# Attention scores as two fp32r passes over high and low parts, queries projected last

## The chip, the cores and the metric

The kernel runs on one core of one Trainium2 chip. The metric is device microseconds (us) of one execution; lower is better. The engines are TensorE (PE in the profile, its weight loads PEld), VectorE (DVE), ScalarE (ACT), GpSimd (POOL) and SyncE (SP), each with a queue of its own that it works through in order; they wait for one another by semaphores. All arithmetic results are float32. "fp32r" is a float32 operand type whose values are first rounded by the engine that writes them; a product that needs full float32 accuracy is built from several fp32r matmuls over a rounded "high" part and the remainder, the "low" part.

## The reference

One encoder layer over 1024 tokens of width 1024: a gated feed-forward half step, a token mixer, and a second feed-forward half step, each with adaptive layer norms. Only the mixer is touched by the change:

```python
proj = u @ w_in                                   # -> qA kA vA | qB kB vB, 8 heads of 64 in A and in B
# A: three dilated windows merged by their softmax denominators, per head a distance penalty
s = q @ k.T * 64 ** -0.5 + bias                   # masked outside the window
o = softmax(s) @ v
# B: 2-D neighbourhood (8 rows x 16 columns of a 16 x 64 grid), learned relative bias
out = concat([yA, yB]) @ w_out
```

## The kernel before, in words

The mixer's attention is one function, `attention_phase`, called twice: stage A for the dilated heads (tag `a`) and stage B for the neighbourhood heads (tag `b`). The eight heads of a stage are four pairs; the two heads of a pair share the 128 partitions, 64 each. A pair has 16 steps (`NU`), one for each of 8 tiles of 128 queries and each head; a stage has 64 steps (`U`).

**Projection.** The queries, keys and values of a pair are six outputs (`outputs`, L1810): part j (0 queries, 1 keys, 2 values) and half of the tokens. Each is 24 fp32r matmuls of 128x512 (`FULL`, L2203), high and low parts of weights and activations. Those of the next pair are spread over the present pair's steps, nine matmuls a step (`SPREAD`). Counting a pair's steps from 0, the outputs end in steps 2, 5, 7, 10, 13 and 15. They lie in two PSUM banks, so that output n+2 may start only when output n has been taken out (`wait_taken`). The last pair projects nothing.

**Taking an output out** (`take`, L1900) is a copy from PSUM by ACT or DVE: each takes one half of keys and values, and each one head of the queries. ACT and DVE do it in the step after the one in which the output ended (`ended_in`). The query buffer `q` holds, for each head, 64 rows of queries and 64 rows of zeros (set by POOL, L1986), so that one 128-row matmul against both heads' keys gives one head's scores. Queries and keys are double-buffered by pair.

**A step u.** PE: `score(u)`, then the transposes of the probabilities of step u-3 (`turn`, L2262), then nine projection matmuls; every eighth step the product with the values (`multiply`, L2288), and in steps 4 to 8 of a pair the transposes of its value tiles (`values`, L2230). In A a score is one float32 matmul of 128x256 over the band of keys (L2243) and four of 32x256 in column tiles of the array (L2246, "128*32" in the profile) for the strided keys `kc`; in B it is one float32 matmul of 128x384 (L2252). The profile shows each float32 matmul as two records. DVE (`step`, L2106): a reciprocal (L2119), bias and minimum (L2124), the normalisation of step u-2 from `ex` into `pn` (L2131), and then what falls due: takes, the low part of a weight (`split`, L2071), value tiles (L2079), output (L2142). ACT: the exponential (L2028, waits for the end of DVE's step), the copy of the turned probabilities of step u-3 (L2036), then takes and the high part of a weight (L2021).

**The entry of a stage** takes the first pair's outputs with nothing else running: values and keys first, then the value transposes, then the queries.

Of the kernel before, what the change touches and what calls it, by code (L numbers as in the profile page):

```python
# [1774 lines left out]
def attention_phase(nc, top, tag, w_in, w_at, w_next, y_at, ut_hi, ut_lo, scratch, ident, bias_in, tab, y_t,  # L1775
# [53 lines left out]
    def taken(n, by_vector):  # L1829

        count = 0
        for m in range(n + 1):
            j, half = outputs(m // NPJ)[m % NPJ]
            count += j == 0 or (half == 0) == by_vector
        return count

    def split_at(g, j):

        return 3 * (g - 1) + ((2, 1, 0) if g == 1 else (1, 0, 2)).index(j) + 1
# [26 lines left out]
    with ExitStack() as st:  # L1866
# [7 lines left out]
        ex = a.sb(tag + "_ex", [P, 2, W])  # L1874
        pn = a.sb(tag + "_pn", [P, 2, W])
# [6 lines left out]
        if dil:  # L1882
            v = a.sb("a_v", [P, S])
            kc = a.sb("a_kc", [P, 2, CL, CK])
            bias = a.sb("a_bias", [P, 2, A_PAD])
            y = a.sb("a_y", [P, S])[:, :]
# [13 lines left out]
        def take(p, i, eng):  # L1900


            on_vector = eng is nc.vector
            copy = nc.vector.tensor_copy if on_vector else nc.scalar.copy
            head = 0 if on_vector else 1
            j, half = outputs(p)[i]
            if j != 0 and half != head:
                return
            eng.wait_ge(pj_mm, NPJ * p + i + 1)
            out = bank(NPJ * p + i)  # L1910
            if j == 0:
                rows = slice(HD * head, HD * head + HD)
                if dil:
                    to = q[rows, p % 2, head, NB * half:NB * half + NB].rearrange("p (t r m) -> p t r m", r=CL, m=CQ)
                    of = out[rows].rearrange("p (t m r) -> p t r m", r=CL, m=CQ)
                else:
                    to = q[rows, p % 2, head, :].rearrange("p (c b r w) -> p c b r w", c=CBS, b=RBS,
                                                           r=QR)[:, :, half]
                    of = out[rows].rearrange("p (r c w) -> p c r w", r=QR, c=CBS)
                if on_vector:  # L1920
                    ins = nc.vector.tensor_scalar(to, of, -HD ** -0.5, None, ALU.mult)
                else:
                    ins = nc.scalar.activation(to, of, ACT.Copy, scale=-HD ** -0.5)
            elif j == 1:
                if dil:
                    m0 = CK // HALVES * half
                    copy(kc[:, p % 2, :, m0:m0 + CK // HALVES], out.rearrange("p (m r) -> p r m", r=CL))
                ins = copy(keys[:, p % 2, NB * half:NB * half + NB], out)
            else:
                if p >= 1:  # L1930
                    eng.wait_ge(v_tr, NVG * p)
                if dil:
                    ins = copy(v[:, NB * half:NB * half + NB], out)
                else:
                    for cb in range(CBS):
                        ins = copy(vc[:, cb, QR * half:QR * half + QR, :],
                                   out.rearrange("p (r c) -> p r c", c=COLS)[:, :, KC0[cb]:KC0[cb] + KC])
            ins.then_inc(pj_v if on_vector else pj_s, 1)

        @block.sync  # L1940
        def _(sp):
# [23 lines left out]
            for p in range(HP):  # L1965
                if p + 2 <= LAST_W:
                    for j in (1, 0, 2):
                        load_part(p + 2, j)
                if p == HP - 1 and ahead is not None:
                    sp.wait_ge(w_lo, split_at(LAST_W, 2))  # L1970
# [12 lines left out]
        def _(pool):  # L1983
            for i in range(2):
                for par in range(2):
                    nc.gpsimd.memset(q[HD * (1 - i):HD * (2 - i), par, i, :], 0.0).then_inc(zeroed, 1)  # L1986
            if dil:
                return
            pool.wait_ge(zeroed, 4)
# [27 lines left out]
        def _(act):  # L2017
# [5 lines left out]
            def exponential(u):  # L2023
# [4 lines left out]
                nc.scalar.activation(ex[:, b, :], t_s[:, b, :], ACT.Exp, bias=sm[:, b, 0:1], scale=-1.0,  # L2028
# [10 lines left out]
            take(0, 2, act)  # L2039
            split(1, 2)  # L2040
            take(0, 3, act)
            split(1, 1)
            take(0, 4, act)
            take(0, 5, act)
            for s in range(U + LAG):
# [5 lines left out]
                for g, i in ended_in(s - 1):  # L2051
                    take(g, i, act)
# [9 lines left out]
                if m == 11 and p + 2 <= LAST_W:  # L2062
                    split(p + 2, 0)
                if m == 0 and 1 <= p and p + 1 <= LAST_W:
                    split(p + 1, 2)

        @block.vector
        def _(dve):
# [37 lines left out]
            def step(u):  # L2106
# [22 lines left out]
                if u >= 4:  # L2129
                    dve.wait_ge(p_tr, u - 3)  # L2130
                nc.vector.tensor_scalar(pn[:, b, :], ex[:, b, :], sm[:, b, 2:3], None,  # L2131
                                        ALU.mult).then_inc(divided, 1)
# [19 lines left out]
            take(0, 0, dve)  # L2152
            take(0, 1, dve)
            split(1, 2)
            for g in range(NVG):
                values(0, g)
            split(1, 1)
            take(0, 4, dve)
            take(0, 5, dve)
            for s in range(U + LAG + 2):  # L2160
# [3 lines left out]
                for g, i in ended_in(s - 1):  # L2164
                    take(g, i, dve)
# [451 lines left out]
```

## Time and profile before

| | us |
|---|---|
| median of 3 runs (2078.32 to 2079.28) | 2078.88 |
| the profiled execution's own time | 2078.98 |
| its span | 2077.2 |
| PE busy | 1959.9 (94%) |
| DVE busy | 1195.8 (58%) |
| ACT busy | 801.3 (39%) |
| stage A, first score to last multiply | 797 to 1050 |
| stage B, first score to last multiply | 1093 to 1300 |

The busy share of PE counts the modelled ends of pipelined matmuls; what a matmul costs in a row of others is the distance between starts. The chain of work that ended last passes through the final feed-forward stage; for the mixer the rows below show which engine the others wait for.

### The profile page before, as it was taken

Reading aid. Unit: us, or ns where it says so; the run is one execution under the profiler, and the core shown is the slowest. Engines: PE = TensorE matmul, PEld = TensorE weight load, DVE = VectorE, ACT = ScalarE, POOL = GpSimd, SP = SyncE. Lnnn points to the kernel's source line nnn. Section 1 sums busy time; section 2 is a strip of 40 time slices with the busy share of each in tenths; the row PEclk is TensorE's granted clock in tenths of the full one; section 3 lists DMA queues with packets and bytes.
Section 4 is the critical chain, followed back from the end, with each engine's and each line's share of the span. In section 5 each row is a group of like instructions: output and inputs, shape, how many; then the busy total and the mean of one; then the engine's idle time right before and its main releaser. Section 6 shows DMA issues by size and latency. Waiting matters only on the chain. (4 is left out here: it accounts for less than half of the span.)

```text
span 2077.2 us, 27306 instructions
## 1 busy us (share of the span) xinstructions
PE 1959.9 (94%) x9962; PEld 1532.6 (74%) x9962; DVE 1195.8 (58%) x2056; ACT 801.3 (39%) x1397; POOL 606.4 (29%) x433
## 2 busy tenths in 40 slices
PE   6899999999999969999889997889999999999996
PEld 4677777777888747777567775778788888887884
DVE  5855555555686963344424445587744444457778
ACT  4533333333445363343413434336433333334541
POOL 0353444333960010000041331001543443449300
PEclk9999999999999989999999999999999999999998
DMA  9255454555874323111042220612233323367732
GB/s 318 64 192 163 163 180 160 179 166 171 317 246 144 101 62 100 30 42 41 11 106 50 41 61 31 233 71 92 95 114 102 108 95 102 117 227 264 251 99 102
DMA packets 184885, 270.56 MB, mean 130 GB/s; under 512 B 12592, under 2 KB 111152, under 8 KB 184624
## 3 DMA queue, kind: packets, MB, share of 16 engines
q1 hardware_dynamic: 153888, 235.18, 33.8%
q10 hardware_dynamic: 29840, 29.50, 4.5%
q0 software_dynamic: 1024, 4.13, 1.2%
q8 instruction: 80, 1.31, 0.3%
q14 instruction: 53, 0.43, 0.1%
HBM read 210.84 MB, written 57.93 MB: 129 GB/s over the span
## 5 line engine op out<-in xcount | busy, mean ns | idle before, releaser
L1581 PE MATMUL f_ps<-f_uh,f_ops 128*128 128x512 f32 x2496 | 783.0, 392 | 13.1 <-DVE f_ops L1272 4.2
L1581 PEld LDWEIGHTS f_ps<-f_uh,f_ops 128*128 128x128 f32 x2496 | 469.6, 188 | 127.5 <-issue 24.1
L1581 PE MATMUL f_ps<-f_ul,f_ops 128*128 128x512 f32 x1248 | 487.6, 391 | 0.0
L966 POOL TENSOR_TENSOR f_sums<-f_raw 128x512 f32<-128x512 f32 x80 | 113.0, 1413 | 547.6 <-DVE f_ul L1401 238.0
L1581 PEld LDWEIGHTS f_ps<-f_ul,f_ops 128*128 128x128 f32 x1248 | 235.0, 188 | 47.6
L1431 DVE TENSOR_TENSOR f_dl<-f_blocks,f_dh 128x1024 fp32r<-128x1024 f32 (+1 forms) x146 | 202.4, 1401 | 81.5 <-ACT f_dh L1162 81.1
L1162 ACT CAST f_dh<-f_blocks 128x1024 fp32r<-128x1024 f32 (+1 forms) x146 | 144.3, 990 | 228.2 <-PE f_ps L1715 225.6
L1715 PE MATMUL f_ps<-f_dh 128*128 128x512 f32 x496 | 196.1, 395 | 9.3 <-DVE f_ev L1465 4.9
L1272 DVE TENSOR_TENSOR f_ops<-f_sums,f_ops 128x512 fp32r<-128x512 f32 x160 | 119.6, 748 | 139.8 <-ACT f_ops L1027 139.7
L1715 PE MATMUL f_ps<-f_dh,f_dl 128*128 128x512 f32 x496 | 194.7, 393 | 0.0
L1715 PE MATMUL f_ps<-f_dl,f_dh 128*128 128x512 f32 x496 | 194.7, 393 | 0.0
L1272 DVE TENSOR_TENSOR f_ops<-f_raw,f_ops 128x512 fp32r<-128x512 f32 x136 | 106.2, 787 | 109.3 <-ACT f_ops L1027 109.2
L2203 PE MATMUL in_pj<-ut_hi,in_wh 128*128 128x512 f32 x360 | 151.6, 421 | 6.7 <-PEq L2583 4.7
L1312 DVE TENSOR_TENSOR acc<-acc,f_ps 128x512 f32<-128x512 f32 x120 | 82.4, 687 | 130.9 <-PE f_ps L1581 130.7
L2203 PE MATMUL in_pj<-ut_hi,in_wl 128*128 128x512 f32 x360 | 142.1, 395 | 0.0
L2203 PE MATMUL in_pj<-ut_lo,in_wh 128*128 128x512 f32 x360 | 141.1, 392 | 0.0
L1715 PEld LDWEIGHTS f_ps<-f_dh 128*128 128x128 f32 x496 | 94.2, 190 | 33.2 <-DVE f_dl L1431 13.8
L1715 PEld LDWEIGHTS f_ps<-f_dh,f_dl 128*128 128x128 f32 x496 | 94.1, 190 | 19.8
L1715 PEld LDWEIGHTS f_ps<-f_dl,f_dh 128*128 128x128 f32 x496 | 94.4, 190 | 19.3
L1027 ACT CAST f_ops<-f_sums 128x512 fp32r<-128x512 f32 x160 | 95.5, 618 | 33.0 <-PE f_ps L1581 17.0
L1027 ACT CAST f_ops<-f_raw 128x512 fp32r<-128x512 f32 x136 | 80.2, 620 | 40.9 <-PE f_ps L1581 17.4
L2028 ACT ACTIVATE a_ex<-a_t,a_sm 128x512 f32<-128x512 f32 x64 | 46.3, 723 | 118.2 <-DVE a_pn L2131 115.3
(249 smaller groups left out, 2987.3 us busy)
## 6 DMA issues: line engine op xcount, KB each, us to landing
f_hidden<-acc SPq DMA_DIRECT2D x154, 256.0 KB, 3.8
f_blocks<-f_hidden SPq DMA_DIRECT2D x154, 256.0 KB, 3.5
f_blocks<-in_ffn_w_down SPq DMA_DIRECT2D x132, 256.0 KB, 6.0
f_raw<-in_ffn_w_gate SPq DMA_DIRECT2D x20, 1024.0 KB, 6.1
f_raw<-in_ffn_w_up SPq DMA_DIRECT2D x20, 1024.0 KB, 5.3
f_aw<-in_w_ada ACTq DMA_DIRECT2D x28, 512.0 KB, 3.6
acc<-in_w_ada ACTq DMA_DIRECT2D x28, 512.0 KB, 4.7
in_raw<-in_w_in SPq DMA_DIRECT2D x24, 512.0 KB, 3.9
```

What stands on the lines that cost most here:

```text
L966: nc.gpsimd.tensor_tensor(sums[:, x], of, with_, how).then_inc(s_done, 1)
L1027: nc.scalar.copy(op(o)[0], source(o)).then_inc(w_hi, 1)
L1162: nc.scalar.copy(high_of(n), operands(n)).then_inc(d_hi, 1)
L1272: nc.vector.tensor_tensor(op(o)[1], source(o), op(o)[0].bitcast(F32), ALU.subtract).then_inc(w_lo, 1)
L1312: nc.vector.tensor_tensor(to, t_in, ps[:, bank, :], ALU.add).then_inc(done, 1)
L1431: nc.vector.tensor_tensor(low_of(n), operands(n), high_of(n).bitcast(F32), ALU.subtract).then_inc(d_lo, 1)
L1581: done = nc.tensor.matmul(ps[:, bank, :], l[:, k, :], r[:, k, :], start=fresh and k == 0 and m == 0, stop=closed and k == HK - 1 and m == ...
L1715: done = nc.tensor.matmul(ps[:, bank(r, t), :], left[m][:, x, P * t:P * t + P], right[m], start=r in OPENS and k == 0 and m == 0, stop=r i ...
L2028: nc.scalar.activation(ex[:, b, :], t_s[:, b, :], ACT.Exp, bias=sm[:, b, 0:1], scale=-1.0, accum_out=sm[:, b, 1:2]).then_inc(exped, 1)
L2203: done = nc.tensor.matmul(bank(n), l[:, k, j, :], r[:, k, NB * half:NB * half + NB], start=y_ == 0, stop=y_ == FULL - 1, skip_group_check= ...
```

## The change

Scores of A's band and of all of B are made of two fp32r matmuls instead of one float32 matmul. With h and l for high and low parts, the first multiplies 128 rows of q_h, stacked twice, with k_h and k_l stacked; the second multiplies the 64 rows of q_l with k_h. For this the keys have, per head, their high part in the head's own 64 rows and their low part in the other 64 (four copies of the keys instead of one, and the scale now sits on the keys); `q` holds the high part twice, and a new `q_lo` the low part of both heads. The 32x256 matmuls of A stay float32 and read a new zero-padded `q_full`. The order of a pair's projection becomes keys, values, queries. The queries are single-buffered. ACT writes the high parts first, DVE then the remainders, one step later than ACT (`ended_in(s - 2)`), and an output counts as taken when both are done. The second score half waits for the second query output separately: at step 8 in A, step 2 in B. The probabilities are normalised in place in `ex`, now three deep, and the exponential waits for the transposes of step u-3; `pn` is gone. The POOL memsets of B go away.

```diff
-        return [(j, half) for j in (1, 0, 2) for half in range(HALVES)]
+        return [(j, half) for j in (1, 2, 0) for half in range(HALVES)]
...
-            count += j == 0 or (half == 0) == by_vector
+            count += j != 2 or (half == 0) == by_vector
...
-        q = a.sb(tag + "_q", [P, 2, 2, S])
-        keys = a.sb(tag + "_k", [P, 2, S])
+        q = a.sb(tag + "_q", [P, 2, S], F32R)
+        q_lo = a.sb(tag + "_q_lo", [P, S], F32R)
+        keys = a.sb(tag + "_k", [P, 2, 2, S], F32R)
...
+                if u >= 3:
+                    act.wait_ge(p_tr, u - 2)
+                nc.scalar.activation(ex[:, u % 3, :], t_s[:, b, :], ACT.Exp, bias=sm[:, b, 0:1], scale=-1.0,
...
+                elif j == 1:
+                    for head in range(2):
+                        ins = nc.scalar.activation(keys[rows_of(head), head, p % 2, key_columns(half)],
+                                                   out[rows_of(head)], ACT.Copy, scale=-HD ** -0.5)
+                    if dil and half == 1:
+                        ins = nc.scalar.activation(class_keys(p, half), class_out(out), ACT.Copy, scale=-HD ** -0.5)
+                    ins.then_inc(pj_s, 1)
+                else:
+                    queries_free(act, p, half)
+                    for head in range(2):
+                        for rows in (rows_of(head), other_rows(head)):
+                            ins = nc.scalar.copy(query_columns(q[rows, head, :], half),
+                                                 query_out(out[rows_of(head)]))
+                    if dil:
+                        ins = nc.scalar.copy(query_columns(q_full[rows_of(1), 1, :], half), query_out(out[rows_of(1)]))
+                    ins.then_inc(pj_s, 1)
...
-                nc.vector.tensor_scalar(pn[:, b, :], ex[:, b, :], sm[:, b, 2:3], None,
-                                        ALU.mult).then_inc(divided, 1)
+                part = ex[:, (u - 2) % 3, :]
+                nc.vector.tensor_scalar(part, part, sm[:, b, 2:3], None, ALU.mult).then_inc(divided, 1)
...
+                dve.wait_ge(pj_s, taken(n, False))
+                for head in range(2):
+                    rows = rows_of(head)
+                    if j == 1:
+                        cols = key_columns(half)
+                        ins = nc.vector.scalar_tensor_tensor(keys[other_rows(head), head, p % 2, cols], out[rows],
+                                                             -HD ** -0.5, keys[rows, head, p % 2, cols].bitcast(F32),
+                                                             ALU.mult, ALU.subtract)
+                    else:
+                        ins = nc.vector.tensor_tensor(query_columns(q_lo[rows, :], half), query_out(out[rows]),
+                                                      query_columns(q[rows, head, :], half).bitcast(F32),
+                                                      ALU.subtract)
...
-            take(0, 0, dve)
-            take(0, 1, dve)
+            take(0, 0)
+            take(0, 1)
             split(1, 2)
+            take(0, 3)
             for g in range(NVG):
                 values(0, g)
...
-                for g, i in ended_in(s - 1):
-                    take(g, i, dve)
+                for g, i in ended_in(s - 2):
+                    take(g, i)
...
                 if m == 0:
+                    wait_taken(output_at(p, 0, 0))
+                if m == (NU // 2 if dil else 2):
                     wait_taken(output_at(p, 0, 1))
...
+                passes = ((slice(0, P), q[:, i, :]), (rows_of(i), q_lo[rows_of(i), :]))
+                for n, (rows, own) in enumerate(passes):
```

PE's queue in one step of stage A, as built before (`a_sc` the scores, `a_tr` the turned probabilities, `in_pj` the projection):

```order
L2243 MATMUL a_sc<-a_k,a_q 128x256
L2246 MATMUL a_sc<-a_kc,a_q 32x256 x4
L2262 MATMUL a_tr<-ident,a_pn 128x128 x4
L2203 MATMUL in_pj<-ut_hi,in_wh 128x512
L2203 MATMUL in_pj<-ut_lo,in_wh 128x512
```

and of the change:

```order
L2306 MATMUL a_sc<-a_k,a_q 128x256
L2306 MATMUL a_sc<-a_k,a_q_lo 128x256
L2316 MATMUL a_sc<-a_kc,a_q_full 32x256 x4
L2325 MATMUL a_tr<-ident,a_ex 128x128 x4
L2263 MATMUL in_pj<-ut_hi,in_wh 128x512
L2263 MATMUL in_pj<-ut_lo,in_wh 128x512
```

One matmul has become two; nothing else moved on PE within the step.

DVE's queue in stage A near the first pair's end, before: the end of step 13, step 14, and the take of the first value half. The queries had been taken four steps earlier:

```order
L2131 TENSOR_SCALAR a_pn<-a_ex,a_sm 128x512
L2119 RECIPROCAL a_sm<-a_sm 128x1
L2124 ISA a_t,a_sm<-a_sc,a_bias 128x512
L2124 ISA a_sm 128x1
L2131 TENSOR_SCALAR a_pn<-a_ex,a_sm 128x512
L1933 COPY a_v<-in_pj 128x512
```

and of the change, from the end of step 15 through steps 0 and 1 of the next pair:

```order
L2162 TENSOR_SCALAR a_ex<-a_ex,a_sm 128x512
L2202 TENSOR_TENSOR a_q_lo<-in_pj,a_q 64x512 x2
L2208 COPY a_q_full<-in_pj 64x512
L2151 RECIPROCAL a_sm<-a_sm 128x1
L2156 ISA a_t,a_sm<-a_sc,a_bias 128x512
L2156 ISA a_sm 128x1
L2162 TENSOR_SCALAR a_ex<-a_ex,a_sm 128x512
L2151 RECIPROCAL a_sm<-a_sm 128x1
L2156 ISA a_t,a_sm<-a_sc,a_bias 128x512
L2156 ISA a_sm 128x1
L2162 TENSOR_SCALAR a_ex<-a_ex,a_sm 128x512
L2202 TENSOR_TENSOR a_q_lo<-in_pj,a_q 64x512 x2
```

The query takes now stand directly ahead of the first score that reads them, and behind ACT's takes of the same outputs, which are these in ACT's queue (the second query output of the pair, then the weight split):

```order
L2064 CAST a_q<-in_pj 64x512 [waits f1_w_hi,f1_lo_b]
L2064 CAST a_q<-in_pj 64x512 x3
L2067 COPY a_q_full<-in_pj 64x512
L2024 CAST in_wh<-in_raw 128x8x128 [waits f1_lo_b,f1_tr]
L2033 ACTIVATE a_ex,a_sm<-a_t,a_sm 128x512 [waits f1_t2,f1_t5,f1_w_lo]
```

Before, ACT had one instruction for its query head there (L1923). Now it has five in A and four in B.

## Rows read from the trace of the kernel before

**Rows 1.** Windows of the two attention stages: each engine's busy time, PEclk, DMA share, GB/s.

```profile
797.00:1046.00 249.00, 237.56 (x1777) 163.25 (x1777) 110.51 (x306) 103.17 (x219) 0.00 (x0) 1.00 0.10 33
1092.00:1301.00 209.00, 195.86 (x1057) 144.16 (x1056) 98.46 (x333) 87.33 (x223) 49.37 (x54) 0.99 0.18 45
```

**Rows 2.** Timeline, one step of stage A: start, length, engine, line, operands.

```profile
855.26 0.59 PE L2243 MATMUL a_sc<-a_k,a_q 128*128 128x256 f32 x2
...
855.78 0.64 PE L2246 MATMUL a_sc<-a_kc,a_q 128*32 128x256 f32 x8
...
856.49 0.16 DVE L2119 RECIPROCAL a_sm<-a_sm 128x1 f32<-128x1 f32 x1 [1.91 <-PE a_sc L2246]
...
857.08 0.39 PE L2203 MATMUL in_pj<-ut_lo,in_wh 128*128 128x512 f32 x1
...
857.31 0.40 PE L2203 MATMUL in_pj<-ut_hi,in_wl 128*128 128x512 f32 x1
...
857.74 0.72 ACT L2028 ACTIVATE a_ex<-a_t,a_sm 128x512 f32<-128x512 f32 x1 [2.38 <-DVE a_pn L2131]
...
858.46 0.56 ACT L2036 COPY acc<-a_tr 128x512 f32<-128x512 f32 x1
...
858.93 0.59 PE L2243 MATMUL a_sc<-a_k,a_q 128*128 128x256 f32 x2
```

**Rows 3.** Timeline, one step of stage B.

```profile
1203.79 0.81 PE L2252 MATMUL b_sc<-b_k,b_q 128*128 128x384 f32 x2
...
1204.44 0.49 PE L2262 MATMUL b_tr<-ident,b_pn 128*128 128x128 f32 x3
...
1205.69 0.62 ACT L2028 ACTIVATE b_ex<-b_t,b_sm 128x384 f32<-128x384 f32 x1
...
1206.31 0.46 ACT L2036 COPY acc<-b_tr 128x384 f32<-128x384 f32 x1
...
1206.83 0.81 PE L2252 MATMUL b_sc<-b_k,b_q 128*128 128x384 f32 x2
```

**Rows 4.** Timeline, the entry of stage A.

```profile
782.55 0.59 ACT L1927 COPY a_kc<-in_pj 128x512 f32<-128x512 f32 x1 [1.66 <-PE in_pj L2203]
782.99 1.29 DVE L2079 COPY acc<-a_tr 128x512 f32<-128x512 f32 x2 [0.84 <-PE a_tr L2230]
783.04 0.59 ACT L1928 COPY a_k<-in_pj 128x512 f32<-128x512 f32 x1
...
797.53 0.67 PE L2243 MATMUL a_sc<-a_k,a_q 128*128 128x256 f32 x2 [0.82 <-DVE a_q L1921]
...
798.70 0.50 PE L2203 MATMUL in_pj<-ut_hi,in_wh 128*128 128x512 f32 x1
```

**Rows 5.** Groups of instructions: count, busy us, mean ns, idle before and its releaser.

```profile
L1312 DVE TENSOR_TENSOR acc<-acc,f_ps 128x512 f32<-128x512 f32 x120 | 82.4, 687 | 130.9 <-PE f_ps L1581 130.7
...
L2021 ACT CAST in_wh<-in_raw 128x1024 fp32r<-128x1024 f32 x21 | 22.2, 1057 | 3.3 <-DMA in_raw<-in_w_in 3.2
...
L1923 ACT ACTIVATE a_q<-in_pj 64x512 f32<-64x512 f32 x8 | 4.7, 592 | 11.7 <-PE in_pj L2203 11.6
...
L2071 DVE TENSOR_TENSOR in_wl<-in_raw,in_wh 128x1024 fp32r<-128x1024 f32 x21 | 26.9, 1282 | 12.5 <-ACT in_wh L2021 12.5
```

**Rows 6.** Timeline, fourth pair of stage A: first score and next multiply.

```profile
997.29 0.59 PE L2243 MATMUL a_sc<-a_k,a_q 128*128 128x256 f32 x2
...
1006.25 3.71 PE L2288 MATMUL mix_o<-acc 128*64 128x128 f32 x56 [0.72 <-ACT acc L2036]
```

**Rows 7.** Timeline, fourth pair of stage B: the same two.

```profile
1257.08 0.81 PE L2252 MATMUL b_sc<-b_k,b_q 128*128 128x384 f32 x2
...
1263.61 4.50 PE L2288 MATMUL mix_o<-acc 128*64 128x128 f32 x32 [0.62 <-ACT acc L2036]
```

**Rows 8.** Timeline, value transposes in step 7 of a pair of stage A.

```profile
893.93 0.75 PE L2230 MATMUL a_tr<-ident,a_v 128*128 128x128 f32 x4 [0.36 <-DVE acc L2079]
```

**Rows 9.** Window of the multiply of rows 7, columns as in rows 1.

```profile
1263.00:1268.00 5.00, 4.39 (x32) 2.99 (x32) 1.81 (x1) 1.26 (x5) 1.59 (x1) 0.66 0.01 3
```

More of the change, by code:

```diff
@@ L1898, in bank @@
             return o[:, 0, :] if bank_of(n) == 2 else pj[:, bank_of(n), :]
[L1900 to L1928, printed above, removed]
-            else:
[L1930 to L1938, printed above, removed]
@@ new lines, in key_columns, with queries_free, take_values @@
+        def key_columns(half):
+            return slice(NB * half, NB * half + NB)
+        def queries_free(eng, p, half):
+            if p >= 1:
+                last = (HT, TT)[half] if dil else (TT - 1, TT)[half]
+                eng.wait_ge(qk, NU * (p - 1) + 2 * last)
+        def take_values(p, half, eng, copy, done):
+            out = bank(output_at(p, 2, half))
+            if p >= 1:
+                eng.wait_ge(v_tr, NVG * p)
+            if dil:
+                ins = copy(v[:, NB * half:NB * half + NB], out)
+            else:
+                for cb in range(CBS):
+                    ins = copy(vc[:, cb, QR * half:QR * half + QR, :],
+                               out.rearrange("p (r c) -> p r c", c=COLS)[:, :, KC0[cb]:KC0[cb] + KC])
+            ins.then_inc(done, 1)
@@ L1940, in _, with class_keys, class_out @@
+        def class_keys(p, half):
+            m0 = CK // HALVES * half
+            return kc[:, p % 2, :, m0:m0 + CK // HALVES]
+        def class_out(out):
+            return out.rearrange("p (m r) -> p r m", r=CL)
         @block.sync
@@ L2150, in output, with take @@
                 ins.then_inc(y_out, 1)
-            take(0, 0, dve)
-            take(0, 1, dve)
+            def take(p, i):
+                j, half = outputs(p)[i]
+                if j == 2 and half == 1:
+                    return
+                n = NPJ * p + i
+                out = bank(n)
+                if j == 2:
+                    dve.wait_ge(pj_mm, n + 1)
+                    take_values(p, half, dve, nc.vector.tensor_copy, pj_v)
+                    return
+                dve.wait_ge(pj_s, taken(n, False))
[10 more added lines that the diff above has]
+                                                      ALU.subtract)
+                if dil and j == 1 and half == 0:
+                    ins = nc.vector.tensor_scalar(class_keys(p, half), class_out(out), -HD ** -0.5, None, ALU.mult)
+                if dil and j == 0:
+                    ins = nc.vector.tensor_copy(query_columns(q_full[rows_of(0), 0, :], half), query_out(out[rows_of(0)]))
+                ins.then_inc(pj_v, 1)
+            take(0, 0)
+            take(0, 1)
             split(1, 2)
+            take(0, 3)
             for g in range(NVG):
```

90 lines of the change are left out of this document (52 added, 38 removed).

## The prediction

> **What bounds the kernel now.** I read the window view by stage first. The change touches only the two attention stages, 249 and 209 us long; PE is busy for 237.6 and 195.9 us of them at full clock, DVE and ACT for less than half [rows 1]. Then the timeline of one step each. In A a step lasts 3.67 us, first score to next score (855.26 to 858.93) [rows 2]; in B 3.04 us [rows 3]. In both, DVE sits idle until PE's scores come (the 1.91 us in brackets) and ACT waits 2.38 us for DVE: for three of four pairs PE sets the pace, and what is taken off a score shortens the step. But ACT and DVE have fixed places in it, and these decide the losses. In A DVE starts 1.23 us after the step's start, ACT at 2.48, and ACT is through with its two fixed instructions at 3.76, already in the next step; DVE's fixed part ends just before ACT starts, at 2.4 [rows 2]. In B ACT runs from 1.90 to 2.98 and DVE is done by 1.9 [rows 3]. In the fourth pair, without projections, the chain PE, DVE, ACT sets the pace [rows 6, 7].
>
> **Gain: the scores.** A 512-column fp32r matmul costs 0.23 us, 857.08 to 857.31 [rows 2], so 0.45 ns a column: 0.115 us for 256 columns, 0.17 for 384. The float32 score of B costs 0.65 us for 384 columns, to the next start [rows 3]; at that rate A's 256 columns are 0.43, but 0.52 us pass before the column-tiled matmuls start [rows 2]. I read the 0.09 us between as the price of changing from the whole array to column tiles. The second new pass has 64 rows, a row tile, between passes over the whole array; no row shows such a change. Bounds: 0, or 0.09 each way. I take 0.09, as the nearest change seen.
> - A: 0.115 + 0.09 + 0.115 + 0.09 = 0.41 instead of 0.52, 0.11 less, times 64 = 7.0 us.
> - B: 0.17 + 0.09 + 0.17 + 0.09 = 0.52 instead of 0.65, 0.13 less, times 64 = 8.3 us.
>
> Sum 15.3 us. In the fourth pairs the score is a link of the chain, so I count all 64. With no row-tile change it would be 0.20 and 0.31 us each, 32.6 us; if a short pass costs as much as a 512-column one (0.23), A pays 0.55 and B 0.46 to 0.64: nothing, about -2 to +12 us.
> The Trainium skill (TensorEngine Tiling, Key Properties) says that changing the tiling mode drains the engine. The 0.09 us at 128*32 agrees with it; that it holds for row tiles no row shows. With the rule the gain is the 15.3 us taken, without it the 32.6.
>
> **Loss: the takes.** A query or key copy costs ACT 0.59 us whether it has 64 or 128 rows [rows 4, 5], and back to back they start 0.49 us apart (782.55, 783.04) [rows 4]. DVE copies go at 1.29 us for two [rows 4], and two-source ones are 0.69 each [rows 5], so 0.65 apiece. ACT's query take grows from one instruction to five in A (4 x 0.49 + 0.59 = 2.55 us) and four in B (2.06); DVE's to three (1.9) and two (1.3), and DVE now starts after ACT. The key take costs 1.1 to 1.6 us on ACT and 1.3 to 1.9 on DVE. For most outputs the next user of the bank comes 24 matmuls later, and the take still ends before it. Not so at these places:
>
> - *Entry of A, 5.0 us.* The value transposes need DVE, whose first value copy stood at 782.99 [rows 4]. Now DVE first takes the second key half, behind ACT: 782.55 + 1.57 + 1.29 = 785.4, so all that follows comes 2.4 later. At the end of the entry, PE's next projection (798.70) needs the bank of the last query output; its take began about 0.8 us before the first score (797.53, after its 0.82 us wait), at 796.75. Now: 796.75 + 2.4 + 2.55 + 1.95 = 803.7, against 798.70.
> - *Entry of B, 1.6 us.* Two ACT copies, not three: 2.0 later. The first score needs only the first query output, so its 0.8 us wait goes (as in [rows 4]); the bank there is another. ACT's and DVE's split of the next weight, queued behind, makes the first transposes wait some 0.4.
> - *Each pair's first score.* The first query output ends in step 13. ACT takes it after its fixed part of step 14, 3.6 us into it, so from 0.1 to 2.65 of step 15; DVE from 2.7 to 4.6, which is 1.1 us into the next pair's step 0, with a step of 3.5. The score waits 1.1 us: twice in A, 2.2 us. In B 2.0, then 3.3 in a step of 2.9: 0.5; and step 2 needs the second query output, which DVE finishes 6.7 us after the pair's start against 6.2: 0.6 more. Twice 1.1 = 2.2 us.
> - *The fourth pairs.* There no projection covers ACT's and DVE's work. In A: first score at 1.1, its exponential and copy to 4.75, query take to 7.3, weight split (1.06 [rows 5]) to 8.35; DVE's take from 7.35 to 9.25, its split (1.2 to 1.3 [rows 5]) to 10.5, then step 2 to 11.65; ACT's exponential and the copy on which the multiply waits end at 13.1. Before, the multiply started 8.96 after the first score [rows 6]: 4.1 us. In B, with four and two copies and no split: 9.5 against 6.53 [rows 7]: 3.0 us.
> - *Step 7.* A value transpose waits 0.36 us for DVE's value copy, which stands behind a weight split [rows 8]; B has the same order. Now two key remainders (1.29 us) stand ahead of both: 1.3 us, in two pairs of each stage, 5.2 us.
> - *Clock, 1 us.* PE now idles some 5 us before A's multiply in the fourth pair. Before B's, where it had been little busy, the granted clock was 0.66 [rows 9], between the levels of 1.2 and 2.4 GHz. A slow multiply of 3.7 us costs 0 to 3 us; I take 1.
>
> Sum: 5.0 + 1.6 + 2.2 + 2.2 + 4.1 + 3.0 + 5.2 + 1 = 24.3 us. The places are queue positions worked out; 15 to 30 covers what I may have misplaced.
>
> **Costed at nothing.** Normalising in place is the same DVE instruction. The exponential's new wait, for the transposes of step u-3, ends before DVE's fixed part does: these follow the score directly on PE, while DVE needs 1.2 us from the score. If they were held up by value copies ahead, ACT and then the copy behind it would slip, a few tenths in five steps of a pair. Without the POOL memsets B's bias loads can only start sooner. The new order of weight parts keeps SP's loads and the splits at the same steps; the query part is needed last and split last. Single-buffered queries cost a wait on scores already done when ACT gets there (step 13's by 15, step 15's by step 0).
>
> **Sum.** The profiled execution took 2078.98 us, 0.1 above the median of 2078.88, with 1.8 us around its span of 2077.2. 2078.98 - 15.3 + 24.3 = 2088.0 us.
>
> **Rivals.**
> 1. *The row tile costs no change, so the gain wins.* 2079.0 - 32.6 + 24.3 = 2070.7, faster. For it: B's score and the next projection are 0.65 us apart, so a change of operand type alone costs nothing [rows 3]. Against it: the 0.09 us at column tiles [rows 2].
> 2. *The short passes gain nothing*, because each needs a weight load that 115 ns of streaming does not hide. 2079.0 - 0 + 24.3 = 2103.3, slower still. For it: the array is loaded once per pass and the only fp32r matmuls here have 512 columns. Against: four transposes, each with a 128-column weight load of its own, start and end within 0.75 us [rows 8].
>    The Trainium skill (TensorE: Matmul & The Clock Gate, LDWEIGHTS) says a load goes by its columns, not its rows, so that the half-height pass loads no faster; no row here shows a 64-row load.
> 3. *The stalls at pair ends and step 7 do not occur* (2.2 + 2.2 + 5.2 = 9.6), the takes ending earlier than I place them: 2088.0 - 9.6 = 2078.4, no change. For it: DVE and ACT have over half of each stage free [rows 1]. Against: free time after the need is no use, and the order of the queues puts the takes just ahead of it.
>
> **Chances.** A difference of under 0.2% (4.2 us: 2074.8 to 2083.1) can't be told from none. Forecast 0.45, its own range 2082 to 2095; rival 1 0.27; rival 2 0.14; rival 3 0.14. Rival 1 ends faster unless the stalls are at their upper end, rival 3 mostly within the bound, the forecast slower but for a tenth of its weight. So faster 0.26, the same 0.18, slower 0.56. The range reaches to rivals 1 and 2: 2069 to 2102.
>
> **What would show it.** The timeline of a step in A: the column-tiled matmuls 0.41 us after the first pass, step 3.56; in B the transposes 0.52 minus the change back, some 0.43, after the first pass, step 2.91. A gap of 0.09 before the 64-row pass speaks for the forecast, none for rival 1, starts 0.2 apart for rival 2. At the entry of A, PE idle for 3.7 us after the first score. At pair starts, PE's first score waiting about 1 us for DVE's query remainder. In the fourth pair of A, 13 us from first score to multiply, less the gain. I am wrong if the steps are shorter by 0.2 us or more, or if the waits for DVE's takes are missing.

## The result and the profile after

The changed kernel takes 2124.53 us, median of 4 runs (2122.67 to 2129.33), against 2079.08 (2078.32 to 2079.68) for the kernel before: ratio 1.0222, 95% interval 1.0205 to 1.024. It is slower by 45 us; the forecast was slower by 9, and the time lies outside the range. The profiled execution took 2122.67 us with a span of 2120.9, so the spans differ by 43.7 us.

First the windows of the two stages, columns as in [rows 1], their edges moved to where the stages now lie.

```profile
797.00:1080.00 283.00, 252.83 (x1863) 177.31 (x1862) 131.10 (x333) 127.09 (x261) 1.99 (x4) 0.97 0.10 30
1114.00:1331.00 217.00, 203.88 (x1014) 145.07 (x1015) 105.70 (x323) 99.81 (x240) 50.65 (x58) 0.94 0.18 43
```

PE is idle for 30 us of stage A's window, 11 before, and the granted clock has fallen from 1.00 and 0.99 to 0.97 and 0.94. The second row is the one to remember: the idle time was forecast, the clock hardly.

Then the timeline of one step in A, the answer to [rows 2], and of one in B, the answer to [rows 3].

```profile
862.13 0.40 PE L2263 MATMUL in_pj<-ut_hi,in_wl 128*128 128x512 f32 x1
862.36 0.28 PE L2306 MATMUL a_sc<-a_k,a_q 128*128 128x256 f32 x1
862.57 0.38 PE L2306 MATMUL a_sc<-a_k,a_q_lo 64*128 64x256 f32 x1
862.88 0.64 PE L2316 MATMUL a_sc<-a_kc,a_q_full 128*32 128x256 f32 x8
...
866.03 0.28 PE L2306 MATMUL a_sc<-a_k,a_q 128*128 128x256 f32 x1
```

```profile
1173.94 0.34 PE L2311 MATMUL b_sc<-b_k,b_q 128*128 128x384 f32 x1
1174.21 0.44 PE L2311 MATMUL b_sc<-b_k,b_q_lo 64*128 64x384 f32 x1
1174.59 0.55 PE L2325 MATMUL b_tr<-ident,b_ex 128*128 128x128 f32 x3
1174.89 0.47 PE L2263 MATMUL in_pj<-ut_hi,in_wh 128*128 128x512 f32 x1
```

In A the two passes take 0.21 + 0.31 = 0.52 us, exactly what the float32 score took, and the step is 3.67 as before. In B they take 0.27 + 0.38 = 0.65, as before too, and the transposes after the 64-row pass 0.30 instead of 0.24: the step is 3.10 against 3.04 (DVE falls behind by 0.06 to 0.07 us with each step). The forecast gain of 15.3 us does not exist. TensorE's weight loads say where it went (the same step, loads only):

```profile
862.13 0.19 PEld L2306 LDWEIGHTS a_sc<-a_k,a_q 128*128 128x128 f32 x1
862.57 0.18 PEld L2306 LDWEIGHTS a_sc<-a_k,a_q_lo 64*128 64x128 f32 x1 [0.25 <-issue]
862.88 0.16 PEld L2316 LDWEIGHTS a_sc<-a_kc,a_q_full 128*32 128x32 f32 x8
```

The full-array pass of 862.36 has its weights loading from 862.13, beside the projection ahead of it. The 64-row pass of 862.57 has its load start at 862.57, with the pass itself.

The waits, where they were forecast. The entry of A (compare [rows 4]): first the value transposes of the kernel before; then, of the changed kernel, DVE's remainder, PE's value transposes, and the first projection of the next pair:

```profile
783.74 2.08 PE L2230 MATMUL a_tr<-ident,a_v 128*128 128x128 f32 x11 [0.35 <-DVE acc L2079]
```

```profile
786.02 1.39 DVE L2198 SCALAR_TENSOR_TENSOR a_k<-in_pj,a_k 64x512 fp32r<-64x512 f32 x2 [2.23 <-ACT a_kc L2058]
...
788.19 2.82 PE L2290 MATMUL a_tr<-ident,a_v 128*128 128x128 f32 x11 [3.17 <-DVE acc L2111]
...
807.44 0.76 PE L2263 MATMUL in_pj<-ut_hi,in_wh 128*128 128x512 f32 x1 [4.19 <-DVE a_q_full L2208]
```

A pair start of A; step 7 of the second pair of A (compare [rows 8]), its transposes; step 7 of a pair of B, its transposes and two projections after them; the fourth pair of A (compare [rows 6]), from its first score to the multiply; the fourth pair of B (compare [rows 7]).

```profile
871.14 0.38 PE L2306 MATMUL a_sc<-a_k,a_q 128*128 128x256 f32 x1 [1.30 <-DVE a_q_full L2208]
...
907.87 0.75 PE L2290 MATMUL a_tr<-ident,a_v 128*128 128x128 f32 x4 [2.03 <-DVE acc L2111]
...
1202.87 0.66 PE L2290 MATMUL b_tr<-ident,acc 128*128 128x128 f32 x4 [1.89 <-DVE acc L2111]
...
1204.63 0.63 PE L2263 MATMUL in_pj<-ut_lo,in_wh 128*128 128x512 f32 x1
1205.06 0.63 PE L2263 MATMUL in_pj<-ut_hi,in_wl 128*128 128x512 f32 x1
```

```profile
1015.61 0.38 PE L2306 MATMUL a_sc<-a_k,a_q 128*128 128x256 f32 x1 [1.29 <-DVE a_q_full L2208]
...
1019.37 2.35 ACT L2064 CAST a_q<-in_pj 64x512 fp32r<-64x512 f32 x4
1021.73 0.58 ACT L2067 COPY a_q_full<-in_pj 64x512 f32<-64x512 f32 x1
...
1022.35 1.39 DVE L2202 TENSOR_TENSOR a_q_lo<-in_pj,a_q 64x512 fp32r<-64x512 f32 x2 [2.67 <-ACT a_q_full L2067]
...
1026.82 1.11 PE L2325 MATMUL a_tr<-ident,a_ex 128*128 128x128 f32 x4 [5.20 <-DVE a_ex L2162]
```

```profile
1292.66 0.45 PE L2311 MATMUL b_sc<-b_k,b_q 128*128 128x384 f32 x1 [0.25 <-DVE b_q_lo L2202]
...
1299.70 0.69 PE L2311 MATMUL b_sc<-b_k,b_q 128*128 128x384 f32 x1 [4.29 <-DVE b_q_lo L2202]
```

And windows around six of these stalls, columns as before:

```profile
786.00:792.00 6.00, 3.81 (x15) 3.27 (x16) 4.97 (x8) 0.93 (x1) 0.00 (x0) 0.72 0.51 212
806.00:813.00 7.00, 5.56 (x20) 3.81 (x21) 2.12 (x7) 2.27 (x4) 0.00 (x0) 0.57 0.01 2
907.00:914.00 7.00, 6.13 (x45) 4.43 (x45) 2.85 (x9) 1.29 (x3) 0.00 (x0) 1.00 0.26 75
1026.00:1033.00 7.00, 5.93 (x61) 4.83 (x61) 1.83 (x7) 2.02 (x5) 0.00 (x0) 0.68 0.01 2
1202.00:1209.00 7.00, 6.13 (x24) 4.48 (x24) 2.56 (x9) 1.07 (x3) 0.00 (x0) 0.76 0.00 1
1299.00:1308.00 9.00, 8.29 (x43) 5.30 (x43) 2.67 (x9) 2.12 (x6) 0.44 (x1) 0.56 0.01 2
```

Five of the six are followed by a stretch at the lower of TensorE's two levels: after 1.89 us of idle in step 7 of B the projections start 0.43 us apart (1204.63, 1205.06) instead of 0.23. The sixth, 2.03 us in step 7 of A (907.87), is not, although it is the longer one: its granted clock is 1.00, and so it is behind the same stall of the next pair (979 to 987 us) and behind the pair start of 871.14. So not every stall brings a slow stretch, and its length alone doesn't say which one does. If the clock is either at its 2.4 or at its 1.2 GHz, a window of length L at mean c has spent 2(1 - c)L at the lower one and lost at most half of that, since what falls into idle time, or where PE isn't the bound, costs nothing: at most 1.7, 3.0, 2.2, 1.7 and 4.0 us here, 12.6 in all. The entry of B (0.79 from 1103 to 1111 us) adds at most 1.7, and the kernel before had 1.7 of this kind ([rows 9]), so at most some 13 us are new.

The shift of DVE's first instruction of each step, changed kernel against the one before, gives a ledger:

| place | forecast, us | measured, us |
|---|---|---|
| ahead of stage A | 0 | +1.6 |
| entry of A | +5.0 | +9.2 |
| A, pairs 1 to 3: scores; pair starts and step 7 | scores: below; +4.8 | +7.6 |
| A, fourth pair | +4.1 | +4.6 |
| entry of B | +1.6 | +3.8 |
| B, pairs 1 to 3: longer step; pair starts and step 7 | scores: below; +4.8 | +3 and +5.8 |
| B, fourth pair | +3.0 | +6.8 |
| behind B | 0 | +1.3 |
| clock | +1 | in the rows above |
| scores | -15.3 | 0, and the +3 of B above |
| sum | +9.0 | +43.7 |

### The profile page after: what moved, and what is told of

Read it like the earlier page. It is cut to its first block and busy times, and to the rows that moved or that the text cites. A ratio compares the mean times of both kernels' runs of the same rounds, so it can differ in the third digit from the quotient of the medians.

```text
span 2120.9 us, 27326 instructions
## 1 busy us (share of the span) xinstructions
PE 1980.1 (93%) x9962; PEld 1545.3 (73%) x9962; DVE 1230.8 (58%) x2104; ACT 846.9 (40%) x1477; POOL 598.7 (28%) x427
## 5 line engine op out<-in xcount | busy, mean ns | idle before, releaser
L2000 POOL DMA_DIRECT2D b_runs<-bias_table x32 | 16.2, 515 | 299.4 <-POOLq L2647 298.6
```

What stands on the lines that cost most here:

```text
L2000: pool.dma_start(runs[QC * rr:QC * rr + QC, :, 0:RUN], tab[:, 2 * p:2 * p + 2, at:at + RUN]).then_inc(r_ld, 16)
```

## The experiments

The ratio of each run is to the kernel before, timed beside it. Differences in us between two runs are those of their medians; worked out from the ratios they come out up to 3 us larger or smaller.

**Two parts of the change alone.** Normalisation in place, on the kernel before:

```diff
-        ex = a.sb(tag + "_ex", [P, 2, W])
-        pn = a.sb(tag + "_pn", [P, 2, W])
+        ex = a.sb(tag + "_ex", [P, 3, W])
...
+                if u >= 3:
+                    act.wait_ge(p_tr, u - 2)
```

> The kernel before with nothing but the normalisation in place: three buffers of exponentials instead of two and two of normalised ones. Theory: this part of the change is worth nothing, 2077-2081. Rival (the exponential waits for the transposes of three steps before, and loses time after a stall, or the engine reads and writes one buffer more slowly): 2084 or more, with ACT's wait for the transposes shown.

Measured 2080.5 us, ratio 0.9999 (0.999 to 1.0009): worth nothing, as expected. The order of the projections, on the kernel before:

```diff
-        return [(j, half) for j in (1, 0, 2) for half in range(HALVES)]
+        return [(j, half) for j in (1, 2, 0) for half in range(HALVES)]
...
-                for g, i in ended_in(s - 1):
+                for g, i in ended_in(s - 2):
                     take(g, i, dve)
```

> The kernel before with float32 scores and double-buffered queries, but the projections of a pair in the order keys, values, queries, and DVE's copies one step later, as in the changed kernel. Theory (the order alone puts the last query copy at the pair's end, but one plain copy on each engine is short): 2079-2085, the pair starts and the fourth pairs together at most 6 us later. Rival (the order alone makes the stalls of the pair starts, of the fourth pairs and of step 7): 2090-2100.

Measured 2080.9 us, ratio 0.9998 (0.9989 to 1.0007). Queries last cost nothing while a take is one instruction per engine. What is left for the 45 us are the scores and the takes: these are longer, DVE's wait for ACT's, and the queries have one buffer. The last point, and POOL's dropped memsets, no run takes by themselves.

**The second pass.** Left out:

```diff
-                passes = ((slice(0, P), q[:, i, :]), (rows_of(i), q_lo[rows_of(i), :]))
+                passes = ((slice(0, P), q[:, i, :]),)
```

> The changed kernel without the second pass: the product of the low parts of the queries with the high parts of the keys is left out, the rest (remainders included) stays. With the run of the second pass over all rows it tells what a pass costs and what the change of rows costs. Theory: a pass over all rows costs 0.11-0.17, so this is a further 0.11 x 64 + 0.17 x 64 = 18 us below the run with whole-array passes, about 2080 (2070-2088); a pass over 64 rows costs 0.31 in A and 0.37 in B. Rival (the score's time isn't on the path): 2118-2126.

Measured 2085.6 us, ratio 1.0024 (1.0015 to 1.0034): 39 us below the changed kernel, for 128 second passes. That is 0.30 us each. In the steps it is more in B than the pass itself: a score falls from 0.52 to 0.21 us in A (855.77 to 855.98 in its trace) and from 0.65 to 0.18 in B (1132.14 to 1132.32), since the first pass then no longer stands before another shape; in the fourth pairs, where PE isn't the bound, it is less.

The pass made over all rows comes next. A form of it with zeros in the other head's rows needs twice the space for the low query parts and did not fit in SBUF, so it has no time. The one below leaves the other head's low parts in place:

```diff
-                passes = ((slice(0, P), q[:, i, :]), (rows_of(i), q_lo[rows_of(i), :]))
+                passes = ((slice(0, P), q[:, i, :]), (slice(0, P), q_lo))
```

> The changed kernel with its second pass over all 128 rows instead of its head's 64, on the same q_lo tile: the other head's rows of q_lo meet this head's low key parts, a product of two remainders some 2^-24 of the score, so nothing is zeroed and nothing else changes. Theory (the change to 64 rows and back and the load that the 64-row pass cannot hide eat what the missing passes save): from the first matmul of a score to its end 0.52 becomes 0.32-0.36 in stage A, 0.64 becomes 0.34-0.42 in stage B; 0.18 x 64 + 0.26 x 64 = 28 us off the changed kernel: 2097 (2090-2104); the one-pass run at 2085.6 leaves 0.11 to 0.17 a pass for it. Rival (a second pass costs 0.3 whatever its rows): 2120-2126.

Measured 2097.1 us, ratio 1.0077 (1.0062 to 1.0092): 27.4 us off the changed kernel by making the matmul twice as tall. It is 11.5 us above the run with one pass, where 18 had been expected; the steps account for some 15 (3.47 against 3.33 in A, 2.76 against 2.59 in B), and the rest is open. Timelines of a step in A, matmuls, then loads, and of one in B:

```profile
855.60 0.28 PE L2306 MATMUL a_sc<-a_k,a_q 128*128 128x256 f32 x1
855.72 0.28 PE L2306 MATMUL a_sc<-a_k,a_q_lo 128*128 128x256 f32 x1
855.92 0.64 PE L2316 MATMUL a_sc<-a_kc,a_q_full 128*32 128x256 f32 x8
...
855.37 0.19 PEld L2306 LDWEIGHTS a_sc<-a_k,a_q 128*128 128x128 f32 x1
855.60 0.19 PEld L2306 LDWEIGHTS a_sc<-a_k,a_q_lo 128*128 128x128 f32 x1
...
1130.68 0.34 PE L2311 MATMUL b_sc<-b_k,b_q 128*128 128x384 f32 x1
1130.86 0.34 PE L2311 MATMUL b_sc<-b_k,b_q_lo 128*128 128x384 f32 x1
1131.04 0.49 PE L2325 MATMUL b_tr<-ident,b_ex 128*128 128x128 f32 x3
```

0.12 + 0.20 = 0.32 in A, 0.18 + 0.18 = 0.36 in B. The load of the second pass now starts 0.12 us ahead of it, and the starts are no further apart than the 0.115 and 0.17 us that the columns take to stream. The first pass of the changed kernel costs 0.09 us more before the 64-row pass (0.21) than before the same pass at full height (0.12), and the pass ahead of the column-tiled matmuls shows that price too (0.20 instead of 0.12). In the other order, on the changed kernel:

```diff
-                passes = ((slice(0, P), q[:, i, :]), (rows_of(i), q_lo[rows_of(i), :]))
+                passes = ((rows_of(i), q_lo[rows_of(i), :]), (slice(0, P), q[:, i, :]))
```

> The changed kernel with its two passes in the other order: the 64-row pass (low query parts by high key parts) first, then the pass over all rows. It tells the two causes of the 64-row pass's price apart. If the price is the change of rows alone (one change in, one out, wherever the pass stands), each score costs the same and the whole is 2122-2126. If it is the weight load that can't be hidden beside a pass of another shape, then the load of the 64-row pass now stands behind the last projection (more idle before the score) and the load of the full pass behind the 64-row pass: the same count of bare loads, 2122-2128 as well, but in A the step from the second pass to the class products falls from 0.31 to 0.22, and the time turns up ahead of the score. Rival (the end of the 64-row pass was slow only because the column-tiled class products or the transposes come next): 5 us or more faster, 2110-2119.

Measured 2144.0 us, ratio 1.0312 (1.0284 to 1.034): 19.5 us slower still, which none of the three foresaw. Its timeline in A, and in B:

```profile
864.67 0.39 PE L2263 MATMUL in_pj<-ut_hi,in_wl 128*128 128x512 f32 x1
864.99 0.38 PE L2306 MATMUL a_sc<-a_k,a_q_lo 64*128 64x256 f32 x1
865.30 0.38 PE L2306 MATMUL a_sc<-a_k,a_q 128*128 128x256 f32 x1
865.61 0.64 PE L2316 MATMUL a_sc<-a_kc,a_q_full 128*32 128x256 f32 x8
...
864.99 0.18 PEld L2306 LDWEIGHTS a_sc<-a_k,a_q_lo 64*128 64x128 f32 x1 [0.35 <-issue]
865.30 0.19 PEld L2306 LDWEIGHTS a_sc<-a_k,a_q 128*128 128x128 f32 x1
...
1162.46 0.44 PE L2311 MATMUL b_sc<-b_k,b_q_lo 64*128 64x384 f32 x1
1162.83 0.45 PE L2311 MATMUL b_sc<-b_k,b_q 128*128 128x384 f32 x1
1163.12 0.49 PE L2325 MATMUL b_tr<-ident,b_ex 128*128 128x128 f32 x3
...
1162.83 0.19 PEld L2311 LDWEIGHTS b_sc<-b_k,b_q 128*128 128x128 f32 x1 [0.19 <-issue]
```

In A the last projection takes 0.32 us to the next start (0.23 otherwise), and both passes take 0.31, each with its load starting together with it, and each before yet another shape. The full pass of B separates the two prices: it is the first of its shape, with its load bare, but the transposes behind it have its shape, and it takes 0.29 us instead of 0.18. So one rule covers the three kernels. A pass costs its streaming, 0.11 us in A and 0.17 to 0.18 in B, where its own load ran ahead and the next instruction has its shape; 0.09 to 0.10 more when the next has another shape; and 0.11 more when it is itself the first of its shape, since its load doesn't run ahead. The 0.31 is 0.11 + 0.11 + 0.09. For A that gives 0.20 + 0.31 = 0.51 in the changed kernel (measured 0.52), 0.11 + 0.20 = 0.31 at full height (0.32) and 0.09 + 0.31 + 0.31 = 0.71 here; for B 0.27 + 0.38 = 0.65 in the changed kernel, behind which the transposes, first of their shape again, take another 0.06. Whether the 0.11 is the bare load or something else in entering a shape, the rows can't tell; the two always come together.

The step is 3.86 us for 3.67 in A and 3.16 for 3.10 in B, 12 of the 19.5 us over 48 steps each; the granted clock of A's window is 0.93 instead of 0.97, and the rest was not taken apart. My miscount was to take the loads as equally many: in A, with the low pass between projection and full pass, two score passes stand bare, not one.

**The takes.** DVE's remainders left out, on the full-height version (low parts stay zero):

```diff
-                for head in range(2):
...
+                if not dil or (j == 1 and half == 1):
+                    dve.wait_ge(pj_v, taken(n, True) - 1)
+                    dve.sem_inc(pj_v, 1)
+                    return
```

> The run with whole-array passes without DVE's remainders: the low parts of keys and queries are zeroed once by POOL and stay zero (the products with low parts are left out in effect), ACT's casts, the float32 copies, both passes, order, banks and waits stay. It tells whether the remainders on DVE or the casts on ACT cost what the stalls cost. Theory (the stalls at the entries, pair starts, step 7 and in the fourth pairs are DVE's 1.4 us remainders in series behind ACT): 20 to 28 us off 2097.1, 2069-2077. Rival (ACT's four casts a query half are what delays, the remainders only happen to end last): at most 10 us off, 2087 or more.

Measured 2071.3 us, ratio 0.9957 (0.9943 to 0.9972): 25.8 us for 64 instructions of 0.69 us, what the waits behind them do to the clock included; of their 44 us of DVE time less than half had been covered. The first of the two entry edits:

```diff
-            take(0, 3)
             for g in range(NVG):
                 values(0, g)
+            take(0, 3)
```

> The run with whole-array passes plus the first of the two entry edits alone: DVE's key remainder of the second half behind its copies of the first value transposes, the banks as in the changed kernel. It divides the 16.2 us that both edits gave. Theory (3.2 us of idle at the value transposes, then some 3.5 us at the lower clock level, and a smaller part in B; the other half is the projection behind the last query take): 6 to 9 us off 2097.1, so 2088-2091. Rival (one of the two edits gives it all): 2096-2097 or 2081-2083.

Measured 2087.0 us, ratio 1.0033 (1.0021 to 1.0046): 10.1 us off, just more than the 6 to 9 expected. Both entry edits:

```diff
-            return (0, 1, 2, 0, 1, 0)[n]
+            return (0, 1, 2, 0, 2, 1)[n]
```

> The run with whole-array passes plus two edits at the entry of a stage: DVE's key remainder of the second half behind its copies of the first value transposes, and the two query projections in the banks 2 and 1 instead of 1 and 0, so that the next pair's first projection waits for an earlier take. Theory (entry A's 9.2 us are the value transposes behind the remainder, the projection behind the last query take, and the cold clock behind each): 7-9 us off in A and 2-3 in B, about 2086 (2084-2090). Rival (the entry is bound by the sum of ACT's and DVE's takes before the first score): at most 3 us off, 2094 or more.

Measured 2080.9 us, ratio 1.0003 (0.9993 to 1.0012): 16.2 us off, more than the 7 to 13 of the expected range. The two waits at the entry of A in the runs with one edit and with both:

```profile
784.61 2.08 PE L2290 MATMUL a_tr<-ident,a_v 128*128 128x128 f32 x11 [0.35 <-DVE acc L2111]
802.82 0.76 PE L2263 MATMUL in_pj<-ut_hi,in_wh 128*128 128x512 f32 x1 [4.39 <-DVE a_q_full L2208]
```

```profile
785.96 2.08 PE L2290 MATMUL a_tr<-ident,a_v 128*128 128x128 f32 x11 [0.35 <-DVE acc L2111]
...
799.68 0.50 PE L2263 MATMUL in_pj<-ut_hi,in_wh 128*128 128x512 f32 x1
```

The first edit takes the 3.17 us before the transposes away, the second the 4.39 before the projection, and the window of 797 to 857 us goes from a granted clock of 0.94 to 1.00. The idle time that the two edits remove at A is 7.2 us; the rest of the 16 must be clock and B's entry, which no run separates. Next, on top of both, DVE's value copies ahead of takes and splits:

```diff
+                if values_due(s - 1):
+                    values(*values_due(s - 1))
                 for g, i in ended_in(s - 2):
                     take(g, i)
```

> The run before this one plus DVE's copies of the value transposes ahead of its takes and weight splits in each step. Theory (the transposes of step 7 wait behind remainder and split, with a cold clock after it): 6 stalls of 1.3 to 1.9 us plus 1 to 2 us of cold clock in some, 6-9 us off the run with the entry edits. Rival (the remainder that is now later is waited for instead, by the projection that needs its bank): no change within 2 us.

Measured 2072.9 us, ratio 0.9959 (0.9944 to 0.9975): 8.1 us off, as expected. And the query projections finished sooner:

```diff
-    SPREAD = 9
+    SPREAD = [9] * 12 + [12] * 3 + [0]
+    DONE = [sum(SPREAD[:m]) for m in range(17)]
```

> The run before this one plus another spread of the projections: 9 matmuls in each of the first 12 steps, 12 in the next three and none in the last, in place of 9 in all 16; the first query half ends a step earlier and the second two steps. Theory (pair starts wait 1.3 us for the first half's remainder, and the fourth pair opens with the last take on ACT and DVE uncovered, 3.6 and 4.4 us of it): 6 x 1.1 = 6 us and 4 to 6 us off, some 10 in all. Rival (the longer steps 12 to 14 and the empty step 15 lose what the takes gain, since the take then stands in a step without projections): within 2 us of the run before, or slower.

Measured 2065.4 us, ratio 0.9927 (0.9911 to 0.9944): 7.5 us off, a little under the 10 expected; PE's wait for the first query remainder at pair starts (1.3 to 1.5 us each) is gone. The control with float32 scores and the same edits (the one on DVE's key remainder has nothing to act on there):

> A control for the four stacked edits: the kernel before with its float32 scores and plain double-buffered copies, the order keys, values, queries, and all the edits of the early-queries run (banks 2 and 1 at the entry, DVE's copies of the value transposes ahead of its takes, the spread 9, 12, 0). Theory (the two passes over all rows are worth some 31 us in the score groups and give back most of it in takes; what the edits gain they gain mostly by hiding those takes): 2073-2079, so the early-queries run's 2065.4 is faster than this one by 8 to 14. Rival (the edits alone are what makes that version fast, and the two passes are worth nothing net): 2062-2067.

Measured 2076.6 us, ratio 0.9989 (0.9979 to 0.9999). So the edits do little for the kernel that has no long takes, and the two passes are worth some 11 us once their second pass is full-height and their takes are covered. Last, the query take divided over two steps, its copies for the other rows read from SBUF:

```diff
+                        for head in range(2):
+                            ins = nc.scalar.copy(query_columns(q[other_rows(head), head, :], half),
+                                                 query_columns(q[rows_of(head), head, :], half).bitcast(F32))
```

> The early-queries run plus a lighter last query take: ACT rounds the two own halves and copies its float32 part, and a semaphore then lets DVE begin, while ACT makes the two copies for the other rows from SBUF, one step later in the loop; DVE's float32 copy comes a step later too. Theory (at the start of the fourth pair nothing covers ACT's 2.9 us and DVE's 2.1 us; steps there wait 4.6 us for DVE in A and 3.1 in B): 1 to 2 us off at each of both fourth pairs and 1 us at each entry, 3 to 5 us in all, 2060-2062. Rival (the copies from SBUF or the later ones are then waited for by the first scores): within 1 us of 2065.4 or slower.

Measured 2062.4 us (2058.3 to 2066.6), ratio 0.9918 (0.9895 to 0.994): the fastest, 0.8% below the kernel before. Its interval overlaps with that of the run before it (0.9911 to 0.9944), so that this last edit gains anything is likely but not shown; the wait it aimed at is shorter in the fourth pair of A (4.64 us in the run before):

```profile
996.96 1.12 PE L2348 MATMUL a_tr<-ident,a_ex 128*128 128x128 f32 x4 [2.76 <-DVE a_ex L2174]
```

## Why the prediction was wrong

The direction was right and the time too low: 2088.0 against 2122.67 us of the profiled execution, 34.7 us. In the ledger's terms 18.3 of them are the scores (15.3 forecast as gained, 3 lost), 13.5 the stalls with the clock behind them, and 2.9 lie ahead of A and behind B, where nothing was forecast.

- **The gain of 15.3 us, the step that failed.** "I take 0.09, as the nearest change seen." What it took is right: the pass before the 64-row one costs 0.21 and not 0.11, and the 64-row pass pays the same again on its own way out. But "0.115 + 0.09 + 0.115 + 0.09 = 0.41" has one price for each change, and there are two. The first matmul of a new shape also starts together with its weight load, and that term, which stands only in rival 2, was put at nothing in the sum. It measures 0.11 us, for the full pass of B in the run with the low pass first (0.29 - 0.18) and for the 64-row pass of A here (0.31 - 0.115 - 0.09). With it the forecast's own sum gives 0.41 + 0.11 = 0.52 in A (measured 0.52) and 0.52 + 0.11 = 0.63 in B (0.65), and B's transposes behind the pass take 0.06 more. That is as much as the passes left out saved: the gain is 0 in A and -3 us in B. The row it came from, [rows 2], could not show it: in the kernel before the only such changes are those to and from the column-tiled matmuls, where such a price would be inside their 0.57 us and the transposes behind. The full-height run shows that nothing else was wrong with the term: a score is 0.20 us shorter in A (0.52 to 0.32) and 0.29 in B (0.65 to 0.36), where 0.20 and 0.31 had been worked out for passes without that change.
- **Rival 2 had the time's reason half right.** Its figure, 2103.3, assumed that any short pass waits for its load. The full-height passes are 0.12 us apart with loads recorded at 0.19, so that is false; here only a load across a change of shape waits. Its chance was put at 0.14, on four transposes of one shape, [rows 8], which say nothing on a change.
- **The stalls and the clock behind them, the other failed step.** The waits stood where they were placed: 3.17 and 4.19 us at the entry of A (2.4 and 2.6 of net delay foreseen), 1.30 at pair starts (1.1), 2.03 in step 7 of A (1.3 and the 0.36 there before) and 1.89 and 0.64 in that of B, and 12.6 from first score to multiply in A's fourth pair (1015.61 to 1028.18; 13 foreseen). But the stalls in the ledger sum to 37.8 us against 23.3 foreseen and 1 for the clock. The largest excesses are the entry of A (4.2), B's fourth pair (3.8) and the entry of B (2.2), and the windows there are at the lower level for a part (0.72 and 0.57, 0.56, and 0.79 from 1103 to 1111 us). I had priced the clock once, at the one place where the kernel before showed it, [rows 9], and not behind every stall that might bring it. The 2.8 us of excess in pairs 1 to 3 of A are not clock, which is at 1.00 behind those waits: they are five shifts of 1.5 us, the fifth the start of the fourth pair, which the forecast had under that pair, and the others each 0.2 to 0.4 longer than foreseen. How the excess at the other places divides between clock and waits is argued from the windows, not measured.
- **Costed at nothing, and right:** the in-place normalisation (ratio 0.9999), the order of projections and DVE's later step (0.9998). What POOL's dropped memsets and the single-buffered queries are worth no run shows.
- **Rivals 1 and 3** fell: no step became shorter, and every forecast wait occurred.

A sum of measured terms, with one remainder: the full-height run has steps 0.20 us shorter in A and 0.28 in B (3.47 and 2.76), 23 us over 48 steps each. Remainders cost 25.8. That leaves 14 for everything else in the change, ACT's casts and the float32 copies above all: -23 + 26 + 14 = +17, the full-height run; +27 for the 64 rows gives +44. The 14 is what is left, not measured by itself.

The Trainium skill (TensorEngine Tiling, Key Properties) says that a change of tiling mode drains the engine; the trace agrees, with 0.09 to 0.10 us on the matmul ahead of the change. A second statement of the Trainium skill (TensorE: Matmul & The Clock Gate, The mechanism) is that a weight load overlaps matmuls under way only when its row group differs; the same section also lets a load into a background weight buffer run ahead. As it stands the "only" doesn't hold here: loads of the same 128*128 shape and the same rows ran ahead of their pass (855.60 for 855.72). The load for the 64-row tile, whose rows are among those of the full-array pass ahead of it, did not (862.57 for 862.57). The measurement decides.

## What to carry to other kernels

A short matmul in another tile shape between full ones pays for the change on both sides and, with its load not running ahead, 0.11 us more: in all 0.20 us a step more than the same matmul padded to the full array where column tiles follow anyway (A), 0.34 where its neighbours are full-array ones on both sides (B). Pad it, with rows whose product is negligible if there are any. Look at the granted clock behind each new stall of PE: several here brought a slow stretch worth up to 4 us, and stalls of 1.3 and 2.0 us none. And put the long take behind the short copy that PE waits for.

## What the runs showed of the hardware

- A 256-column fp32r pass over the whole array costs 0.11 to 0.12 us among its like; one over 64 rows between other shapes 0.31, nearly three times as much for half the rows.
- In the run with the low pass first, both passes of A cost 0.31, the 64-row one and the full one: it is the change that counts, not the height. Leaving a shape costs 0.09 to 0.10 us, entering one 0.11 (0.29 instead of 0.18 for the full pass of B), or 0.06 where three transposes follow (0.30 instead of 0.24).
- After 1.89 us of PE idle behind a stretch of normal work, the projections from 1204.63 on ran at half speed up to the next score (1208.04); after 2.03 us of it (907.87, 980.11) none did.
- With the normalisation in place alone, the exponential waited for the transposes of three steps before twice, 0.9 and 0.8 us of ACT, and the kernel's time stayed the same (0.9999).
